# The rotary columns of a latent attention projected twice, with halves exchanged, in a one-core decoder step

## The reference

```python
def rope(x, pos):
    half = ROPE_DIM // 2
    inv = jnp.exp(-math.log(ROPE_THETA) * jnp.arange(half, dtype=jnp.float32) / half)
    ang = pos.astype(jnp.float32)[:, None] * inv[None, :]
    cos = jnp.cos(ang)[None, :, None, :]
    sin = jnp.sin(ang)[None, :, None, :]
    x1, x2 = xf[..., :half], xf[..., half:]
    return jnp.concatenate([x1 * cos - x2 * sin, x2 * cos + x1 * sin], axis=-1)

def mla_project(c_q, c_kv, k_pe, pos, q_norm, w_uq, kv_norm, w_uk):
    q = (rms_norm(c_q, q_norm) @ w_uq).reshape(b, s, MLA_HEADS, NOPE_DIM + ROPE_DIM)
    q_nope = q[..., :NOPE_DIM]
    q_pe = rope(q[..., NOPE_DIM:], pos)
    k_pe = rope(k_pe[:, :, None, :], pos)[:, :, 0]
    ckv = rms_norm(c_kv, kv_norm)
```

## Time and profile before

| | us |
|---|---|
| median of 3 runs | 2348.23 |
| lowest and highest | 2346.67 and 2349.3 |
| the profiled execution | 2344.28 |
| its span, first to last instruction | 2342.6 |
| granted TensorE clock over the span | 0.955 of full |

### The profile page before, as it was taken

The page is one execution under the profiler, slowest core; times in us unless marked ns, Lnnn a source line. Parts: engine busy times, 40 slices in busy tenths (PEclk is TensorE's granted clock), DMA queues, the critical chain, the costliest instruction groups (busy, mean ns, idle before and its releaser), DMA issues.

```text
span 2342.6 us, 41476 instructions
## 1 busy us (share of the span) xinstructions
PE 2204.5 (94%) x16722; PEld 2079.0 (89%) x16722; DVE 1029.6 (44%) x1279; ACT 699.7 (30%) x897; POOL 279.7 (12%) x289
## 2 busy tenths in 40 slices
PE   7999999998999999999999999998864599999997
PEld 7999999995999999999999999996520289999997
DVE  5442445466544334464433446665510054433443
ACT  5431222234254222234412222222510025522221
POOL 1001002100410000030000013030025240000002
PEclk9999999997999999999999999999975689999999
DMA  3244222220232222322222223233177322232221
GB/s 123 90 100 122 90 90 90 99 94 1 67 108 93 91 77 90 101 68 92 89 91 81 90 96 94 87 62 92 47 208 215 92 91 90 81 99 81 90 96 68
DMA packets 69014, 217.80 MB, mean 93 GB/s; under 512 B 10733, under 2 KB 23213, under 8 KB 68848
## 3 DMA queue, kind: packets, MB, share of 16 engines
q1 hardware_dynamic: 59440, 191.91, 25.3%
q0 software_dynamic: 9488, 24.71, 4.2%
HBM read 211.88 MB, written 5.71 MB: 93 GB/s over the span
## 4 chain that ended last, share of the span: by engine, by line
PE 86%; DVE 4%; DMA 3%; issue 3%; ACT 2%; SPq 2%; POOLq 1%; POOL 0%; DVEq 0%; ACTq 0%
PE ps L546 80%; DMA raw<-down 1%; SPq L444 1%; DVE rinv L1241 1%; PE ps L844 1%; DMA raw<-w_uq 1%; DVE w_lo L1231 1%; SPq L426 1%; PE ps L782 1%; POOLq L426 1%; DMA keys<-pool_kt 1%; ACT prob L1062 1%; ACT p_mla L1159 0%; PE ps L634 0%; PE ps L795 0%
## 5 line engine op out<-in xcount | busy, mean ns | idle before, releaser
L546 PE MATMUL ps<-hx_hi,w_hi 128*128 128x272 f32 x3376 | 702.7, 289 | 15.4 <-DVE hx_lo L1252 13.0
L546 PE MATMUL ps<-hx_hi,w_lo 128*128 128x272 f32 x3376 | 699.6, 289 | 0.0
L546 PE MATMUL ps<-hx_lo,w_hi 128*128 128x272 f32 x3376 | 696.9, 288 | 0.0
L995 ACT ACTIVATE w_hi<-raw 128x1024 fp32r<-128x1024 f32 (+2 forms) x299 | 334.7, 1119 | 1204.8 <-PE ps L546 1171.7
L546 PEld LDWEIGHTS ps<-hx_hi,w_hi 128*128 128x128 f32 x3376 | 531.8, 188 | 19.4 <-issue 14.4
L546 PEld LDWEIGHTS ps<-hx_lo,w_hi 128*128 128x128 f32 x3376 | 531.5, 189 | 0.0
L546 PEld LDWEIGHTS ps<-hx_hi,w_lo 128*128 128x128 f32 x3376 | 527.9, 189 | 0.0
L1231 DVE TENSOR_TENSOR w_lo<-raw,w_hi 128x1024 fp32r<-128x1024 f32 (+2 forms) x299 | 420.7, 1407 | 126.0 <-ACT w_hi L995 125.8
L546 PE MATMUL ps<-hid_hi,w_hi 128*128 128x272 f32 x1408 | 292.2, 289 | 4.1 <-DVE w_lo L1231 4.1
L546 PE MATMUL ps<-hid_lo,w_hi 128*128 128x272 f32 x1408 | 291.9, 288 | 0.0
L546 PE MATMUL ps<-hid_hi,w_lo 128*128 128x272 f32 x1408 | 291.5, 288 | 0.0
(11 more groups left out here) (277 smaller groups left out, 1619.7 us busy)
## 6 DMA issues: line engine op xcount, KB each, us to landing
raw<-gu SPq DMA_DIRECT2D x176, 512.0 KB, 3.2
raw<-down SPq DMA_DIRECT2D x64, 704.0 KB, 4.0
keys<-pool_kt SPq DMA_DIRECT2D x128, 144.0 KB, 3.7
vals<-pool_v POOLq DMA_DIRECT2D x128, 128.0 KB, 3.3
raw<-odd_in SPq DMA_DIRECT2D x21, 512.0 KB, 3.2
raw<-even_in SPq DMA_DIRECT2D x14, 512.0 KB, 3.2
raw<-even_out SPq DMA_DIRECT2D x8, 512.0 KB, 3.2
raw<-odd_out SPq DMA_DIRECT2D x8, 512.0 KB, 3.2
```

The lines of the kernel that those rows point to most:

```text
L546: last = pe.matmul(acc[slot][0:m, a, 0:TH], w, r[:, t, a * TH:(a + 1) * TH], start=(begin and t == tiles[0] and one == 0), stop=(end and t ...
L995: act.activation(w_hi[slot][:, 0:cols], raw[slot][:, 0:cols], ACT.Copy).then_inc(w_hi_done, 1)
```

## The change

The exchange of halves is moved into the weights. Each query panel gets 32 more columns: the head's rotary columns once more, with the halves exchanged, so that one panel of 128 columns gives the head (96) and its turned rotary part (partitions 96 to 127, `QK:P`). The fourth copy in the key's panel is exchanged too. The sign moves into the table `sin`. `perm`, `rotate` and the semaphore `rotated` go.

DVE multiplies the turned part by `sin` from PSUM partitions 96 to 127 to `silu` partitions 64 to 95, and adds. `gate` on the rotary partitions is multiplied by `cos` once, and `sin` by the scale once, so that the eviction itself does the product with `cos`. The key is rotated in the pass of panel `KPE`, ahead of the first query. `acc_read` is given by the second product, and the addition stands behind the split. A query panel's load has 384 KB instead of 288 KB.

```diff
@@ TensorE @@
-                    panel(n, n % 2, cq_hi, cq_lo, range(QT), split_cq if h == 0 else None, m=QK)
+                    panel(n, n % 2, cq_hi, cq_lo, range(QT), split_cq if h == 0 else None)
                     if h == 0:
                         pe.wait_ge(rms_done, stat(4) + 1)
                         stats(sumsq_steps(4) + QT + KT)
-                        pe.wait_ge(spare_landed, 48)
-                        pe.wait_ge(acc_read, KPE + 1)
-                        rotate(kpe, 0)
-                    else:
-                        pe.wait_ge(acc_read, n)
-                        if h == 1:
-                            pe.wait_ge(kpe_done, 1)
-                        else:
-                            pe.wait_ge(q_done, h - 1)
-                        rotate(qf[:, h - 1, :], h)
                 pe.wait_ge(ckv_done, KT)
                 nope_keys(0)
                 nope_keys(1)
-                pe.wait_ge(acc_read, ODD_OUT)
-                pe.wait_ge(q_done, HEADS - 1)
-                rotate(qf[:, HEADS - 1, :], HEADS)
                 nope_keys(2)
                 nope_keys(3)
...
@@ DVE @@
-            def rope(t2d, count):
-
-                r = slice(NOPE, QK)
-                dve.wait_ge(rotated, count)
-                dve.tensor_tensor(halves(silu[r, :]), ps[r, 6:8, 0:TH], halves(sin[r, :]), ALU.mult)
-                link(dve.tensor_tensor(prod[r, :], t2d, cos[r, :], ALU.mult))
-                return dve.tensor_tensor(t2d, prod[r, :], silu[r, :], ALU.add)
+            def rope(t2d):
+
+                r, turned = slice(NOPE, QK), slice(QK, P)
+                link(dve.tensor_tensor(silu[r, :], t2d[turned, :], sin[turned, :], ALU.mult))
+                link(dve.tensor_tensor(t2d[r, :], t2d[r, :], cos[r, :], ALU.mult))
+                return dve.tensor_tensor(t2d[r, :], t2d[r, :], silu[r, :], ALU.add)
...
+                        if n == KPE:
+                            dve.wait_ge(spare_landed, 48)
+                            dve.wait_ge(square_done, sumsq_steps(4) + QT)
+                            dve.wait_ge(acc_read, n + 1)
+                            rope(kpe).then_inc(kpe_done, 1)
                 for h in range(HEADS):
                     n = ODD_UQ + h
+                    if h == 0:
+                        link(dve.tensor_tensor(sin[QK:P, :], sin[QK:P, :], gate[QK:P, :], ALU.mult))
+                        link(dve.tensor_tensor(gate[NOPE:QK, :], gate[NOPE:QK, :], cos[NOPE:QK, :], ALU.mult))
+                    if h:
+                        dve.wait_ge(q_done, h)
+                    else:
+                        dve.wait_ge(kpe_done, 1)
                     dve.wait_ge(panel_done, n + 1)
-                    dve.tensor_tensor(halves(qf[0:QK, h, :]), acc_of(n % 2, QK), halves(gate[0:QK, :]), ALU.mult).then_inc(acc_read, 1)
+                    dve.tensor_tensor(halves(qf[0:QK, h, :]), acc_of(n % 2, QK), halves(gate[0:QK, :]), ALU.mult)
+                    dve.tensor_tensor(halves(silu[NOPE:QK, :]), ps[QK:P, 2 * (n % 2):2 * (n % 2) + 2, 0:TH], halves(sin[QK:P, :]), ALU.mult)\
+                       .then_inc(acc_read, 1)
                     split_next(n)
-                    if h == 0:
-                        dve.wait_ge(spare_landed, 48)
-                        rope(kpe[NOPE:QK, :], 1).then_inc(kpe_done, 1)
-                    else:
-                        rope(qf[NOPE:QK, h - 1, :], h + 1).then_inc(q_done, 1)
+                    dve.wait_ge(acc_read, n + 1)
+                    dve.tensor_tensor(qf[NOPE:QK, h, :], qf[NOPE:QK, h, :], silu[NOPE:QK, :], ALU.add).then_inc(q_done, 1)
...
@@ host @@
+    turned = np.r_[ROPE // 2:ROPE, 0:ROPE // 2]
+    order = np.concatenate(tiles + [np.arange(3 * c_w, k0)] + [np.arange(k0, k0 + ROPE)] * 3 + [k0 + turned])
+    heads = [np.r_[h * QK:(h + 1) * QK, h * QK + NOPE + turned] for h in range(HEADS)]
+    a["w_uq"] = panels(i["mla_w_uq"][0][:, np.concatenate(heads)])
```

More of the change, by code:

```diff
@@ L211, in decoder_step @@
         w_uv = put("w_uv", [P, KT, HEADS * VD])
-        perm = put("perm", [P, ROPE])
         conv_w = put("conv_w", [P, 3, CT])
@@ L345, in decoder_step @@
         ckv_done = sem("ckv_done")
-        rotated = sem("rotated")
         q_done = sem("q_done")
@@ L419, in decoder_step @@
         EVEN_LOADS = 16 * (1 + 4 + 7 + 4)
-        ODD_LOADS = 16 * (8 + CT)
+        ODD_LOADS = 16 * (7 + CT)
         def panel_cols(n):
-            return PANEL_K[n] * (QK if ODD_UQ <= n < ODD_OUT else P)
+            return PANEL_K[n] * P
         def page_numbers(eng, at):
@@ L745, in even @@
                 mixer_out(EVEN_OUT, SGU_TILES, SWA_TILES, EVEN_PIECES)
[L747 to L752, removed]
             def nope_keys(p):
@@ L1623, in odd @@
                                                      op0=ALU.mult, op1=ALU.mult).then_inc(ckv_done, 1)
-                rope(qf[NOPE:QK, HEADS - 1, :], HEADS + 1).then_inc(q_done, 1)
                 mla_maxima(0)
@@ L1746, in _ @@
             pool.wait_ge(stored_even, 16 * 5)
-            for t, name in ((w_uk, "w_uk"), (w_uv, "w_uv"), (perm, "perm"), (conv_w, "conv_w"), (q_gain, "q_gain"), (kv_gain, "kv_gain"),
+            for t, name in ((w_uk, "w_uk"), (w_uv, "w_uv"), (conv_w, "conv_w"), (q_gain, "q_gain"), (kv_gain, "kv_gain"),
                             (causal, "causal"), (causal_s, "causal_s")):
@@ L1791, in rope_tables @@
     cos, sin = (np.tile(f(ang).astype(np.float32), (2, 1)) for f in (np.cos, np.sin))
[L1792 to L1796, removed]
+    sin[:half] *= -1.0
+    return cos, sin
 def constants():
@@ L1808, in constants @@
     c["onehot"] = (bucket[None, :] == np.arange(BUCKETS + 1)[:, None]).astype(np.float32)
-    cos, sin, swap = rope_tables()
-    pad = lambda a: np.concatenate([np.zeros((NOPE, a.shape[1]), np.float32), a, np.zeros((P - QK, a.shape[1]), np.float32)])
-    c["cos"], c["sin"], c["perm"] = pad(cos), pad(sin), pad(swap)
+    cos, sin = rope_tables()
+    c["cos"] = np.concatenate([np.zeros((NOPE, T), np.float32), cos, np.zeros((P - QK, T), np.float32)])
+    c["sin"] = np.concatenate([np.zeros((QK, T), np.float32), sin])
     q = np.arange(P)
@@ L1874, in layout @@
     k0 = 3 * c_w + Q_LORA + KV_LORA
-    order = np.concatenate(tiles + [np.arange(3 * c_w, k0)] + [np.arange(k0, k0 + ROPE)] * 4)
+    turned = np.r_[ROPE // 2:ROPE, 0:ROPE // 2]
+    order = np.concatenate(tiles + [np.arange(3 * c_w, k0)] + [np.arange(k0, k0 + ROPE)] * 3 + [k0 + turned])
     a["odd_in"] = panels(w[:, order])
     a["odd_out"] = panels(i["odd_w_out"][0])
-    a["w_uq"] = panels(i["mla_w_uq"][0], QK)
+    heads = [np.r_[h * QK:(h + 1) * QK, h * QK + NOPE + turned] for h in range(HEADS)]
+    a["w_uq"] = panels(i["mla_w_uq"][0][:, np.concatenate(heads)])
     a["q_gain"], a["kv_gain"] = features(i["mla_q_norm"][0]), features(i["mla_kv_norm"][0])
```

## The result

| | before | after |
|---|---|---|
| median, us | 2348.44 (6 runs) | 2336.94 (6 runs) |
| lowest and highest | 2346.67 and 2351.28 | 2332.44 and 2341.06 |
| the profiled execution, its span | 2344.28, 2342.6 | 2339.13, 2337.5 |
| granted clock over the span | 0.955 | 0.951 |

The ratio is 0.9949, with an interval of 0.9934 to 0.9964: 11.5 us by the medians, 8.5 to 15.5 by the interval. The forecast was 8.8 us, so 2339.4. So faster, and within the range.

A forecast was written before the change was run, and what follows sets the result against it. TensorE's own work (86% of what ended last) was taken as the bound. Restart 2.55, beat 5.15 and key projections 1.1 sum to 8.8 us, taken from the median 2348.23: 2339.4 us, range 2336.4 to 2346.0.

The forecast's parts named there:

- The restart: Head 3's panel, after waiting for its late load, starts 3.55 us earlier; after the clock loss the lead is 2.55 us.
- the open point: Whether head 3's load, now 384 KB, lands as late as before; no delay was taken as likeliest, at most 4.4 us.
- rival A: Head 3's larger load lands later, by 2.7 us, at most 4.4: 2342.1 us, at most 2343.8; chance 0.25.
- The half clock: After standing still, TensorE runs at clock 0.50; 3.1 to 3.2 us lost as before, now all within head 3's panel.
- the drain: While POOL's convolution-state store lands (22.1 us), all queues together move 36 GB/s, against 249 afterwards; it delays head 3's load.
- The beat: Regular alternation on TensorE of a 4.67 us panel and a 1.03 us rotation; removing five rotations saves 5.15 us.
- The key projections: The rotation between the two halves of the key projection goes, saving 1.1 us with its gap.
- The first two rotations: The key's and head 0's run before the late load lands; removing them only adds 2.1 us idle time, worth nothing.
- DVE's cover: DVE needs four operations, 3.1 us a head, against TensorE's 4.67, the turned product at 0.72; nothing is late.
- rival C: The partition-shifted product makes DVE the bound, late from 2.3 us each; at 5 us each 2354.8 us; chance 0.04.
- both slacks are 1.2 us: Behind the late load, w_lo of heads 4 and 5 is ready 1.2 us before TensorE wants each panel.
- a panel of heads 4 to 7 waits for w_lo: Listed sign of a wrong forecast; expected instead were panels of heads 4 to 7 back to back at 4.67 us.

The follow-up runs named there:

- after_again: The changed kernel measured a second time without an edit: 2338.91 us against 2348.07, ratio 0.9955.
- before_again: The kernel before measured again without an edit: 2347.64 us against 2346.63, ratio 1.0015.
- before_wide: The kernel before with query panels of 128 columns (32 unused) and 384 KB loads, rotations kept on TensorE: 2350.84 us, ratio 1.0019.
- after_narrow: The changed kernel with 96-column query panels and 288 KB loads, the exchange of halves left out of the result: 2335.31 us, ratio 0.9943.
- after_packed: The changed kernel with the convolution state copied by POOL to a contiguous tile and stored in 128 pieces of 256 bytes: 2327.67 us, ratio 0.9921.
- before_packed: The kernel before with the convolution state copied by POOL to a contiguous tile and stored in 128 pieces of 256 bytes: 2340.64 us, ratio 0.9974.
- after_warm: The changed kernel with ten idle 32x32 fp32 matmuls on TensorE behind head 2's panel, where it waits for head 3's load: stage 56.10 us, one execution.
- after_warm128: The changed kernel with 42 idle full-size (128x128) matmuls on TensorE behind head 2's panel, where it waits for head 3's load: stage 55.72 us, one execution.
- warm128_halves: The changed kernel with 42 idle full-size matmuls behind head 2's panel and DVE's reciprocal cut in two halves: stage 54.91 us, one execution.

## Why the prediction was right

Its sum was 8.8 us; the stage gave 0.94 + 5.29 + 1.50 = 7.7 (8.0 in after_again; 7.0 and 7.3 against the stage of before_again), the medians 11.5 and 9.2. Term by term, from the first query panel:

- **The restart: forecast 2.55, measured 0.94.** The step that failed is the open point, "I take no delay as the likeliest": head 3's load took 18.7 us, 2.5 more, close to rival A's 2.7. before_wide and after_narrow show that the size alone does it. The prediction weighed the Trainium skill's "DMA: Bandwidth & Descriptors" there, its section on queues, rings and completion order (an engine alternates between queues packet by packet). The measurement went the other way than I had concluded from it. The longer rows weren't more packets by the profile's count (59440 on this queue in before and in before_wide), so the number of turns doesn't decide here. The other reading, 96 KB more at the drain's 36 GB/s, gives 2.7 us and comes close; what holds a longer row up is not shown.
- **The half clock: forecast 3.15 us lost within the panel of head 3, measured 2.0 (1.4 in after_again).** That panel took 6.55 us with 4.51 at full clock; 0.28 us of waiting for w_lo followed. The lead at its start therefore kept whole to its end (0.94 and 0.94), where the forecast gave away 1.0. Together with the late load the restart was mis-sized by 1.6. How much is lost varies without any change: the same panel took 6.84 us in before and 5.90 in before_again.
- **The beat: forecast 5.15, measured 5.3** (from the second line of the table to the third, 23.83 less 18.54). Here two errors nearly cancel. A rotation with a panel behind it is worth 1.19 (5.70 less 4.51) and not 1.03, so the five, four of them with a panel behind, are 5.8; the four panels, at 18.55 us instead of 4 x 4.51 = 18.04, take 0.5 back. About half of that is the halt in front of head 5. The 4.51 could have been had beforehand: 96 matmuls in 12.03 us are 4.51 us for 36, and the forecast kept 4.67 for panels that stand back to back.
- **The key projections: forecast 1.1, measured 1.5** (from the third line to the fourth, 9.67 less 8.17). The two halves take 3.63 and 3.65 us around a rotation and 6.88 in one piece: again more than the rotation's own row.
- **The first two rotations worth nothing:** right while the load is late. after_packed shows the other side: the stage gains 9.95 us once nothing is late.
- **DVE's cover.** The turned product took 0.728 us, the unshifted one 0.72, so rival C is out. The Trainium skill's "Vector Engine (DVE) Microarchitecture Reference", section on the reshape front-end, has such a move as free, and the trace agrees to 0.01 us. The four operations of a head were as forecast. But "both slacks are 1.2 us" rested on the long half clock: w_lo of head 4 ended at 1594.96, 6.8 us after w_lo of head 3 (forecast 6.7), and TensorE wanted it 0.3 us sooner. At full clock it would have wanted it 2.3 us sooner (by the 4.51 us of a panel). The second slack was gone too: head 5's panel waited some 0.2 us for its w_lo. That a panel of heads 4 to 7 waits for w_lo was on the prediction's own list of signs that it is wrong; it came true, at a price of about half a microsecond. The slack was borrowed from the very loss that I counted beside it.

The right total is thus partly luck in its parts: rival A was true, and cost less than its price since the clock came back sooner, and when it comes back varies between executions of one program. What remains open is the gap between the 7.0 to 8.0 us of the stage and the 11.5 and 9.2 of the medians. The intervals (8.5 to 15.5, and 7.5 to 13.9) reach down to about the stage's value. The gap has the same sign between before_packed and after_packed, 9.95 in the stage and 13.0 by the medians. The part behind the scores took between 297.4 and 302.5 us in the fourteen traces (twelve of the experiments, and those of before and after), without an order by kernel. The first query panel started at 1563.2 to 1566.4 us with the old order and at 1563.2 to 1568.4 with the new, and from the next feed-forward layer to the end all fourteen took 413.9 to 414.7 us. So I found no second mechanism; none is shown to be absent.

## What to carry to other kernels

Price an operation on the bound engine by the period with and without it (5.70 against 4.51), not by its own row: its neighbour's restart belongs to it. A slack that was worked out while the bound engine runs slowly is no slack; work it out again at full clock before you count on it. And look at what a late transfer waits for: here a 32 KB store in 8-byte pieces, off every chain, cost 7 us before the change and 9 to 11 after it by the medians, about as much as the whole change brought.

## What I had not expected of the hardware

- A store of 32 KB in 4096 pieces took 20.6 to 22.1 us and held a weight load back from about 3 us to between 16 and 19. The same 32 KB in 128 pieces took 3.3 to 4.0 us, with 0.29 us of copying on POOL.
- In that drain a load of 384 KB took 17.4 to 19.4 us, one of 288 KB 16.2 to 16.9.
- The granted clock fell to 0.50 at 1583.6 in after_warm while the profile shows TensorE busy with 32x32 fp32 matmuls. With 42 full-size ones it stayed at 1.00 in after_warm128, and in warm128_halves it fell 0.9 us after the restart.
- After the restart the clock was at half for 2.9 to 6.8 us, in different executions of nearly the same code.
